# A two-block transformer kernel: one fewer expert round goes through scratch, and the sums read back are added ahead of the last round

## The chip, the core and the metric

The kernel runs on one core of one Trainium2 chip. The metric is the device time of one execution in microseconds (us), lower is better. Engines are called PE (TensorE), ACT (ScalarE), DVE (VectorE), POOL (GpSimd) and SP (SyncE, which here only issues transfers).

## The reference, cut to what matters

Two transformer blocks over 256 tokens of width 1024. The change lies in the last part of the second block, a mixture of experts: every token picks 2 of 32 experts, each expert is a small gated network, and the two results are added with their weights.

```
def hier_moe(h, w_rg, b_rg, w_re, b_re, w1e, w3e, w2e):
    ...
    out = jnp.zeros_like(t)
    for e in range(N_EXPERTS):
        he = jax.nn.silu(t @ w1e[e]) * (t @ w3e[e])
        out = out + cw[:, e:e + 1] * (he @ w2e[e])
    return out.reshape(bsz, seq, d)
```

Behind it stand only `x = x + gt2 * moe`, a last norm (`modulate(rmsnorm_2(x, g_final), shf, scf)`) and the output.

## The kernel before, in words

The 512 (token, expert) pairs are sorted by expert. They are worked off in 20 **rounds** (`NR`), two experts of up to 64 pairs at a time, in the order of the table `ROUNDS`; rounds whose entry is 16 or more take what did not fit into an expert's first 64. A round's weights are six tiles of 1 MB (three for the entry 19): four for gate and up, two for down. They stream from HBM into 15 places, nearly all through SP's queue, in the order of `expert_loads`; a tile is issued when PE has read what lay in its place.

For round i PE makes **gate/up** in two halves (`pe_gate_up`, line 2939, 16 matmuls each), ACT the silu and DVE the product, PE **turns** the hidden tile (`pe_turn_hidden`, line 2961), ACT copies it, and PE makes the **down** product (`pe_down`, line 2973) into two PSUM banks. PE's order interleaves the rounds: first half of i, turn of i-1, second half of i, down of i-1.

What follows a down product depends on `SENT`:

- Rounds below `SENT` go through **scratch**. ACT and DVE copy the two banks to SBUF (lines 3021 and 3066), POOL scatters the rows to a table `Z` in HBM (line 3143; `slot_rows` in the profile), one row per pair. At the end SP reads the whole table back in two transfers (the **readback**, line 3128, into `ZB[0]` and `ZB[1]`, part of the big tile `AR`). ACT multiplies `ZB[0]` by the first weight (line 3053), DVE adds `ZB[1]` times the second (line 3103), and `pe_tokens` (line 2996, 32 matmuls) adds these sums into the PSUM banks of the result.
- Rounds from `SENT` on never leave the core. ACT and DVE make the weighted high and low part of the output (`OHL`, lines 3031 and 3072), DVE a selection matrix (`RT` in the tile `GT`, line 3091), and `pe_back` (line 2984, 16 matmuls) adds the rows to the result's banks.

`ZB` lies where two weight places were, so the readback waits until PE has read the first half of round 18, and for all scatters. Behind the last `pe_back`, DVE adds the result to the residual (line 3299), and the last norm follows. Each engine runs its instructions in the order written, and a wait holds all that is written behind it on that engine. The last round is number 19; "gate/up 19" and so on name its parts.

Of the kernel before, what the change touches and what calls it, by code (L numbers as in the profile page):

```python
# [6 lines left out]
ALU = mybir.AluOpType  # L7
ACT = mybir.ActivationFunctionType
# [26 lines left out]
ROUNDS = (0, 1, 2, 3, 16, 4, 5, 6, 17, 7, 8, 9, 18, 10, 11, 12, 19, 13, 14, 15)  # L35
NR = len(ROUNDS)
WSLOTS = 15
SENT = 17


def tiles(i):
# [164 lines left out]
def build(nc, W, S, K, XI, POS, OUT):  # L206
    with ExitStack() as ctx:
# [72 lines left out]
        p_gu, a_silu, v_mul, a_ah, v_al, p_dn, p_res, v_x = signals("p_gu a_silu v_mul a_ah v_al p_dn p_res v_x")  # L280
# [37 lines left out]
        p_mr, v_mr, a_mr, g_mr = signals("p_mr v_mr a_mr g_mr")  # L318
# [10 lines left out]
        d_zero, d_back = d_ring[2], d_ring[3]  # L329
# [200 lines left out]
        def pe_last_norm(pe, q):  # L530
            q.wait_ge(a_os, SENT + 2 * (NR - SENT))
            q.wait_ge(v_os, SENT + 2 * (NR - SENT))
            for k in range(8):
# [1998 lines left out]
        st8 = get(8 * 2).rearrange("p (n a) -> p n a", a=2)  # L2532
# [42 lines left out]
        ZB = [AR[:, o:o + SLOT].rearrange("p (a d) -> p a d", a=2) for o in (4096, 6144)]  # L2575
# [3 lines left out]
        U0, D0 = 88, 84  # L2579
        row0 = rows.index(("moea", 0))  # L2580
        loads = expert_loads()
        zeroed, back = [16 * sum(1 for s in range(len(order)) if s % RING == b) for b in (2, 3)]
# [360 lines left out]
        def out_read(q, i, n):  # L2943

            if i < SENT:
                q.wait_ge((a_os, v_os)[n], i + 1)
# [4 lines left out]
        def turned(i):  # L2951

            return 4 if i == NR - 1 else 6

        def pe_turn_hidden(pe, q, i):

            q.wait_ge(v_mul, U0 + i + 1)
            if i and turned(i) == 6:
                out_read(q, i - 1, 0)
            for c in range(2):  # L2960
                m = pe.transpose(ps[:, turned(i), c * 128:c * 128 + 128], HID[:, i % 2, c * 128:(c + 1) * 128], ident)
            m.then_inc(*q.up(p_th))

        def pe_down(pe, q, i):

            q.wait_ge(a_ah, U0 + i + 1)
            w = weights(q, i, 2)
            for n in range(2):
                if i:
                    out_read(q, i - 1, n)  # L2970
                for c in range(2):
                    for j in tiles(i):
                        m = pe.matmul(ps[64 * j:64 * j + 64, 6 + n, :], HT[:, i % 2, c, 64 * j:64 * j + 64], w[j][:, c * 1024 + n * 512:c * 1024 + n * 512 + 512],  # L2973
                                      start=c == 0, stop=c == 1, skip_group_check=True)
                m.then_inc(*q.up(p_dn))
# [15 lines left out]
        def pe_tokens(pe, q):  # L2991

            for a in range(2):
                q.wait_ge(v_mr, 12 + a)
                for c in range(8):
                    pe.matmul(half_bank(0, c)[:, 128 * a:128 * a + 128], ZB[0][:, a, c * 128:(c + 1) * 128], ident, start=False, stop=False, skip_group_check=True)

        def pe_experts(pe, q):
            pe_gate_up(pe, q, 0, 0)
            pe_gate_up(pe, q, 0, 1)  # L3000
            pe_rows(pe, q)
            for i in range(1, NR):
                pe_gate_up(pe, q, i, 0)
                pe_turn_hidden(pe, q, i - 1)
                if i - 2 >= SENT:
                    pe_back(pe, q, i - 2)
                pe_gate_up(pe, q, i, 1)
                pe_down(pe, q, i - 1)
            pe_turn_hidden(pe, q, NR - 1)
            pe_back(pe, q, NR - 2)  # L3010
            pe_down(pe, q, NR - 1)
            pe_tokens(pe, q)
            pe_back(pe, q, NR - 1)

        def act_expert_out(act, q, i):
# [17 lines left out]
        def act_experts(act, q):  # L3033
            for i in range(NR + 2):
                if i >= 2:
                    act_expert_out(act, q, i - 2)
                if i + 1 < NR:
                    act_tokens(act, q, i + 1, 0, 8)
                if 1 <= i <= NR:
                    u = i - 1  # L3040
                    q.wait_ge(p_th, u + 1)
                    if u >= 2:
                        q.wait_ge(p_dn, D0 + 2 * (u - 2) + 2)
                    act.activation(acc[:, u % 2, :], ps[:, turned(u), 0:256], ACT.Copy).then_inc(*q.up(a_ah))
                if i < NR:
                    q.wait_ge(p_gu, U0 + 2 * i + 2)
                    if i >= 2:
                        q.wait_ge(p_th, i - 1)
                    act.activation(HID[:, i % 2, :], ps[:, 4 + i % 2, 0:256], ACT.Silu).then_inc(*q.up(a_silu))  # L3049
                if i == NR:  # L3050
                    for a in range(2):
                        q.wait_ge(d_back, back + 32)
                        act.activation(ZB[0][:, a, :], ZB[0][:, a, :], ACT.Copy, scale=st8[:, 6, a:a + 1]).then_inc(*q.up(a_mr))
                if i == 0:
                    q.wait_ge(d_zero, zeroed + 16)
                    for n, x in enumerate((S12, C12)):
                        q.wait_ge(p_mr, 4 + n)
                        act.activation(x, ps[:, n, :], ACT.Copy).then_inc(*q.up(a_mr))
# [16 lines left out]
        def dve_round(v, q, i):  # L3075

            r = ROUNDS[i]
            q.wait_ge(a_mr, 4)
            q.own()
            v.tensor_scalar(EQ, S12, idv[:, r:r + 1], None, ALU.is_equal).then_inc(*q.up(v_own))  # L3080
            q.own()
            if i < SENT:
                v.tensor_tensor_reduce(out=EQ, in0=EQ, in1=slot1, scale=1.0, scalar=0.0, op0=ALU.mult, op1=ALU.add, accum_out=zrow[:, i:i + 1]).then_inc(*q.up(v_own))
                q.own()
                v.tensor_scalar(zno[:, i:i + 1], zrow[:, i:i + 1], 0.0, 4096.0, ALU.is_equal, ALU.mult).then_inc(*q.up(v_own))
                q.own()
                v.scalar_tensor_tensor(out=zidx[:, i:i + 1], in0=zno[:, i:i + 1], scalar=-1.0, in1=zrow[:, i:i + 1], op0=ALU.add, op1=ALU.add).then_inc(*q.up(v_rm))
                return
            if i >= SENT + 2:
                q.wait_ge(p_sc, i - SENT - 1)  # L3090
            v.tensor_tensor(RT[:, i % 2, :], EQ[:, 0:256], EQ[:, 256:512], ALU.add).then_inc(*q.up(v_rm))
            q.wait_ge(a_mr, 5)
            q.own()
            v.tensor_tensor_reduce(out=EQ, in0=EQ, in1=C12, scale=1.0, scalar=0.0, op0=ALU.mult, op1=ALU.add, accum_out=M[:, r:r + 1]).then_inc(*q.up(v_rm))

        def dve_experts(v, q):
            for i in range(NR + 2):
                if i >= 2:
                    dve_expert_out(v, q, i - 2)
                if i == NR:  # L3100
                    for a in range(2):
                        q.wait_ge(a_mr, 6 + a)
                        v.scalar_tensor_tensor(out=ZB[0][:, a, :], in0=ZB[1][:, a, :], scalar=st8[:, 7, a:a + 1], in1=ZB[0][:, a, :], op0=ALU.mult, op1=ALU.add).then_inc(*q.up(v_mr))
                if i == 0:
                    q.wait_ge(a_silu, U0 + 1)
                    v.tensor_tensor(HID[:, 0, :], HID[:, 0, :], ps[:, 4, 256:512], ALU.mult).then_inc(*q.up(v_mul))
                    dve_round(v, q, 0)
                elif i < NR:
                    dve_round(v, q, i)
                    q.wait_ge(a_silu, U0 + i + 1)  # L3110
                    v.tensor_tensor(HID[:, i % 2, :], HID[:, i % 2, :], ps[:, 4 + i % 2, 256:512], ALU.mult).then_inc(*q.up(v_mul))  # L3111

        def sync_experts(sp_, q):

            for m, (i, x, j) in enumerate(loads):
                r = ROUNDS[i]
                if r < PAIRS:
                    place_free(q, m)
                    if i >= 3:
                        q.wait_ge(*read(i - 3, x))  # L3120
                    sp_.dma_start(place(m), W[row0 + 3 * (2 * r + j) + x]).then_inc((d_wa, d_wb, d_wd)[x][i % 3], 16)
                if m == 4:
                    q.wait_ge(g_mr, 1)
                    sp_.dma_start(Z.rearrange("(p a) (b d) -> p (a b) d", p=P, b=2), zeros.unsqueeze(1).broadcast_to([P, 8, 512])).then_inc(d_zero, 16)
            q.wait_ge(p_gu, U0 + 2 * (SENT + 1) + 1)
            q.wait_ge(d_sent, 16 * SENT)
            for c in range(2):
                sp_.dma_start(ZB[c], Z[c * T:(c + 1) * T].rearrange("(a p) d -> p a d", a=2)).then_inc(d_back, 16)
# [340 lines left out]
```

## Time and profile before

| | |
|---|---|
| median of 3 runs | 1602.01 us (1597.74, 1602.01, 1602.54) |
| profiled execution, its time | 1597.53 us |
| profiled execution, its span | 1595.7 us |
| PE busy | 1532.6 us, 96% |
| DVE, ACT, POOL busy | 1057.4, 749.0, 47.9 us |

The span runs from the first to the last instruction, and all times below count from its start. PE's clock is told as granted share of full speed: 1.00 is 2.4 GHz and 0.50 is 1.2 GHz. The change touches only the last 60 us or so.

### The profile page before, as it was taken

The numbers are of one execution on the slowest core, as the hardware profiler recorded it, in microseconds if no ns is written. First come the engines' busy times: TensorE is split into PE (matmuls) and PEld (weight loads), VectorE is DVE, ScalarE is ACT, GpSimd is POOL, SyncE is SP. The second block draws the span as 40 slices with busy tenths as digits, with TensorE's granted clock in tenths as the row PEclk, the third lists the DMA queues.
The fourth block names the chain that finished last, engine by engine and source line by source line (L and its number), as shares of the span: only waits on it lengthen the run. The fifth ranks groups of instructions, "written<-read, shape, count | busy, mean of one in ns | idle before, by whom it ended". The sixth has DMA issues, their size and how long they took to land.

```text
span 1595.7 us, 29188 instructions
## 1 busy us (share of the span) xinstructions
PE 1532.6 (96%) x12098; PEld 1324.7 (83%) x12098; DVE 1057.4 (66%) x2091; ACT 749.0 (47%) x1552; POOL 47.9 (3%) x62
## 2 busy tenths in 40 slices
PE   7999999999999999999989999999999999998897
PEld 7999987889999999998879999999979894332234
DVE  7677775787877787778787787777796546221223
ACT  7455465565444554546365544464744233221124
POOL 0000001000000000000000000000000000222100
PEclk9999999999999999999999999999999999999998
DMA  9746643044666456655314656634410197999993
GB/s 357 282 165 259 263 186 132 1 185 167 244 260 268 174 210 265 263 223 237 122 57 192 240 220 272 251 131 176 147 48 3 54 369 296 417 416 417 418 420 162
DMA packets 55140, 357.75 MB, mean 224 GB/s; under 512 B 9653, under 2 KB 9909, under 8 KB 13152
## 3 DMA queue, kind: packets, MB, share of 16 engines
q1 hardware_dynamic: 48960, 344.92, 54.3%
q0 software_dynamic: 5472, 9.11, 1.5%
q8 instruction: 95, 1.56, 0.4%
q10 hardware_dynamic: 576, 1.86, 0.3%
q14 instruction: 37, 0.30, 0.1%
HBM read 365.64 MB, written 12.06 MB: 237 GB/s over the span
## 4 chain that ended last, share of the span: by engine, by line
PE 82%; DMA 7%; DVE 6%; ACT 3%; issue 1%; SPq 0%; ACTq 0%; DVEq 0%; POOLq 0%
PE ps L433 21%; PE ps L434 21%; PE ps L435 21%; PE ps L2939 5%; DMA AR<-in_w 5%; PE ps L2973 2%; DMA AR<-slot_rows 1%; PE ps L2115 1%; PE ps L1186 1%; ACT SQ L1120 1%; DVE WL L420 1%; PE ps L2687 1%; DVE HL L638 1%; PE ps L1098 1%; PE ps L1153 1%
## 5 line engine op out<-in xcount | busy, mean ns | idle before, releaser
L433 PE MATMUL ps<-HH,WH 128*128 128x256 f32 x1696 | 480.1, 283 | 16.4 <-DVE WL L420 11.6
L420 DVE TENSOR_TENSOR WL<-ring,WH 128x512 fp32r<-128x512 f32 x728 | 451.1, 685 | 52.0 <-ACT WH L409 44.9
L434 PE MATMUL ps<-HL,WH 128*128 128x256 f32 x1696 | 477.9, 282 | 0.0
L435 PE MATMUL ps<-HH,WL 128*128 128x256 f32 x1696 | 477.9, 282 | 0.0
L409 ACT ACTIVATE WH<-ring 128x512 fp32r<-128x512 f32 x728 | 395.5, 621 | 88.1 <-PE ps L435 65.8
L433 PEld LDWEIGHTS ps<-HH,WH 128*128 128x128 f32 x1696 | 320.0, 189 | 19.4 <-DVE HL L638 14.5
L434 PEld LDWEIGHTS ps<-HL,WH 128*128 128x128 f32 x1696 | 320.0, 189 | 0.1
L435 PEld LDWEIGHTS ps<-HH,WL 128*128 128x128 f32 x1696 | 319.9, 189 | 0.0
L433 PE MATMUL ps<-AH,WH 128*128 128x256 f32 x704 | 198.4, 282 | 0.2 <-DVE AL L810 0.2
L434 PE MATMUL ps<-AL,WH 128*128 128x256 f32 x704 | 198.1, 281 | 0.0
L435 PE MATMUL ps<-AH,WL 128*128 128x256 f32 x704 | 198.1, 281 | 0.0
L767 ACT ACTIVATE AF<-AF 128x256 f32<-128x256 f32 x86 | 35.9, 417 | 286.6 <-DVE AF L806 286.6
L433 PEld LDWEIGHTS ps<-AH,WH 128*128 128x128 f32 x704 | 132.5, 188 | 0.5 <-DVE AL L810 0.4
L434 PEld LDWEIGHTS ps<-AL,WH 128*128 128x128 f32 x704 | 132.5, 188 | 0.0
L435 PEld LDWEIGHTS ps<-AH,WL 128*128 128x128 f32 x704 | 132.5, 188 | 0.0
L806 DVE TENSOR_TENSOR AF<-ps,RS 128x512 f32<-128x512 f32 x86 | 59.5, 692 | 50.9 <-PE ps L435 45.0
L3111 DVE TENSOR_TENSOR HID<-HID,ps 128x256 f32<-128x256 f32 x19 | 8.0, 421 | 102.5 <-ACT HID L3049 102.5
L808 DVE TENSOR_TENSOR AF<-AF 128x256 f32<-128x256 f32 x86 | 36.6, 425 | 46.1 <-ACT AF L767 46.1
L2939 PE MATMUL ps<-AR 128*64 128x512 f32 x240 | 65.9, 596 | 0.0
L2939 PE MATMUL ps<-AR,XWR 128*64 128x512 f32 x224 | 62.5, 596 | 2.8 <-DMA AR<-in_w 2.3
L810 DVE TENSOR_TENSOR AL<-AF,AH 128x256 fp32r<-128x256 f32 x86 | 36.6, 425 | 41.6 <-ACT AH L771 41.6
L2973 PE MATMUL ps<-AR,acc 128*64 128x512 f32 x216 | 59.7, 603 | 4.4 <-DMA AR<-in_w 4.4
(565 smaller groups left out, 2189.9 us busy)
## 6 DMA issues: line engine op xcount, KB each, us to landing
ring<-in_w SPq DMA_DIRECT2D x248, 1024.0 KB, 6.9
AR<-in_w SPq DMA_DIRECT2D x70, 1024.0 KB, 20.7
cols<-in_s SPq DMA_DIRECT2D x1, 2994.0 KB, 12.7
SQ<-in_w SPq DMA_DIRECT2D x4, 512.0 KB, 6.4
slot_rows<-RG SPq DMA_DIRECT2D x1, 2048.0 KB, 21.3
AR<-slot_rows SPq DMA_DIRECT2D x2, 1024.0 KB, 19.7
cons<-in_k ACTq DMA_DIRECT2D x1, 1634.0 KB
XT<-in_x SPq DMA_DIRECT2D x2, 512.0 KB
```

Of the source, the lines that this page charges most:

```text
L409: act.activation(hi(n)[:, c * 512:c * 512 + 512], ring[:, i % RING, c * 512:c * 512 + 512], ACT.Copy).then_inc(*q.up(a_wh))
L420: ins = v.tensor_tensor(lo(n)[:, s], ring[:, i % RING, s], hi(n)[:, s].bitcast(F32), ALU.subtract)
L433: pe.matmul(out, ah, bh, start=start, stop=False, skip_group_check=skip)
L434: pe.matmul(out, ah, bl, start=False, stop=False, skip_group_check=skip)
L435: return pe.matmul(out, al, bh, start=False, stop=stop, skip_group_check=skip)
L638: ins = v.scalar_tensor_tensor(out=HL[:, k, :], in0=XT[:, k, :], scalar=gain[:, k:k + 1], in1=HH[:, k, :].bitcast(F32), op0=ALU.mult, op1= ...
L767: act.activation(AF[:, si, 0, :], AF[:, si, 0, :], ACT.Silu).then_inc(*q.up(a_silu))
L806: v.tensor_tensor(AF[:, si], ps[:, b, :].rearrange("p (a t) -> p a t", a=2), RS[:, :].unsqueeze(1).broadcast_to([P, 2, T]), ALU.mult).then ...
L808: v.tensor_tensor(AF[:, si, 0, :], AF[:, si, 0, :], AF[:, si, 1, :], ALU.mult).then_inc(*q.up(v_mul))
L810: v.tensor_tensor(AL[:, si, :], AF[:, si, 0, :], AH[:, si, :].bitcast(F32), ALU.subtract).then_inc(*q.up(v_al))
L2939: m = pe.matmul(ps[64 * j:64 * j + 64, 4 + i % 2, :], XWR[i % 2][:, k, 64 * j:64 * j + 64], w[j][:, (k % 4) * 512:(k % 4) * 512 + 512], st ...
L2973: m = pe.matmul(ps[64 * j:64 * j + 64, 6 + n, :], HT[:, i % 2, c, 64 * j:64 * j + 64], w[j][:, c * 1024 + n * 512:c * 1024 + n * 512 + 512 ...
```

## The change

`SENT` falls from 17 to 16, so round 16 takes the path of `pe_back`. `pe_tokens` is written ahead of the turn of round 19 in PE's program. ACT's two multiplications of `ZB[0]` move from behind the last copy of a turned tile to ahead of the silu of round 19, and DVE's two additions from behind the outputs of round 18 to ahead of the product of round 19. The readback's wait for PE is written in another way and has the same value; its wait for the scatters is for 16 in place of 17.

```diff
-SENT = 17
+SENT = 16
...
             for i in range(1, NR):
...
+            pe_tokens(pe, q)
             pe_turn_hidden(pe, q, NR - 1)
             pe_back(pe, q, NR - 2)
             pe_down(pe, q, NR - 1)
-            pe_tokens(pe, q)
             pe_back(pe, q, NR - 1)
...
+                if i == NR - 1:
+                    for a in range(2):
+                        q.wait_ge(d_back, back + 32)
+                        act.activation(ZB[0][:, a, :], ZB[0][:, a, :], ACT.Copy, scale=st8[:, 6, a:a + 1]).then_inc(*q.up(a_mr))
                 if i < NR:
                     q.wait_ge(p_gu, U0 + 2 * i + 2)
...
                     act.activation(HID[:, i % 2, :], ps[:, 4 + i % 2, 0:256], ACT.Silu).then_inc(*q.up(a_silu))
-                if i == NR:
-                    for a in range(2):
-                        q.wait_ge(d_back, back + 32)
-                        act.activation(ZB[0][:, a, :], ZB[0][:, a, :], ACT.Copy, scale=st8[:, 6, a:a + 1]).then_inc(*q.up(a_mr))
...
-                if i == NR:
-                    for a in range(2):
-                        q.wait_ge(a_mr, 6 + a)
-                        v.scalar_tensor_tensor(out=ZB[0][:, a, :], in0=ZB[1][:, a, :], scalar=st8[:, 7, a:a + 1], in1=ZB[0][:, a, :], op0=ALU.mult, op1=ALU.add).then_inc(*q.up(v_mr))
...
                 elif i < NR:
                     dve_round(v, q, i)
+                    if i == NR - 1:
+                        for a in range(2):
+                            q.wait_ge(a_mr, 6 + a)
+                            v.scalar_tensor_tensor(out=ZB[0][:, a, :], in0=ZB[1][:, a, :], scalar=st8[:, 7, a:a + 1], in1=ZB[0][:, a, :], op0=ALU.mult, op1=ALU.add).then_inc(*q.up(v_mr))
                     q.wait_ge(a_silu, U0 + i + 1)
...
-            q.wait_ge(p_gu, U0 + 2 * (SENT + 1) + 1)
+            q.wait_ge(p_gu, U0 + 2 * (NR - 2) + 1)
             q.wait_ge(d_sent, 16 * SENT)
```

PE at the end of its program: the turn (L2961), `pe_back` (L2984), down (L2973) and `pe_tokens` (L2996) of the last rounds, as a difference.

```order
 L2939 MATMUL ps<-ring,XWR 64x512 x8
 L2973 MATMUL ps<-AR,acc 64x512 x8
+L2996 MATMUL ps<-cons,AR 128x128 x16
 L2961 MATMUL ps<-cons,HID 128x128 x2
 L2984 MATMUL ps<-GT,OHL 128x256 x16
 L2973 MATMUL ps<-AR,acc 64x512 x8
-L2996 MATMUL ps<-cons,AR 128x128 x16
 L2984 MATMUL ps<-GT,OHL 128x256 x16
 L536 MATMUL ps<-cons,SQ 128x1 x16
```

The tokens' matmuls now stand ahead of the turn, the `pe_back` of round 18 and the down product of round 19; before, they stood behind all three.

ACT at the same place, before and then with the change: silu (`HID<-ps`), outputs (`OHL`), copy of a turned tile (`acc`), multiplication of what was read back (`AR<-AR 128x1024`).

```order
L3044 ACTIVATE acc<-ps 128x256
L3049 ACTIVATE HID<-ps 128x256
L3031 ACTIVATE OHL<-ps,AR 128x512 x2
L3044 ACTIVATE acc<-ps 128x256
L3053 ACTIVATE AR<-AR 128x1024 x2
L3031 ACTIVATE OHL<-ps,AR 128x512 x2
L542 ACT_TABLE_LOAD
```

```order
L3044 ACTIVATE acc<-ps 128x256
L3048 ACTIVATE AR<-AR 128x1024 x2
L3053 ACTIVATE HID<-ps 128x256
L3031 ACTIVATE OHL<-ps,AR 128x512 x2
L3044 ACTIVATE acc<-ps 128x256
L3031 ACTIVATE OHL<-ps,AR 128x512 x2
L542 ACT_TABLE_LOAD
```

The pair that waits for the readback now stands ahead of the silu of round 19 (L3053 with the change, L3049 before), of the outputs of round 18 and of the copy of the last turned tile; before, only the outputs of round 19 stood behind it.

The third place is PE's program at round 18, where round 16's `pe_back` is new.

```order
 L2939 MATMUL ps<-AR 64x512 x8
 L2961 MATMUL ps<-cons,HID 128x128 x2
+L2984 MATMUL ps<-GT,OHL 128x256 x16
 L2939 MATMUL ps<-AR 64x512 x8
 L2973 MATMUL ps<-ring,acc 64x512
```

It stands between the halves of gate/up 18, ahead of the down product of round 17.

## Rows read from the trace of the kernel before

**Rows 1.** The page: DMA share and GB/s in 40 slices.

```profile
DMA  9746643044666456655314656634410197999993
GB/s 357 282 165 259 263 186 132 1 185 167 244 260 268 174 210 265 263 223 237 122 57 192 240 220 272 251 131 176 147 48 3 54 369 296 417 416 417 418 420 162
```

**Rows 2.** The chain that ended last, in order: start, us, what.

```profile
1543.88 7.26 DMA slot_rows<-SENDS,AR
...
1551.65 21.82 DMA AR<-slot_rows
1573.47 0.02 issue
1573.50 1.16 ACT AR L3053
1574.65 0.02 issue
1574.68 1.29 DVE AR L3103
1575.97 0.04 issue
1576.02 3.84 PE ps L2996 x32
1579.86 0.48 PE ps L2984 x4
1580.34 0.02 issue
1580.36 0.89 DVE XT L3299 x2
```

**Rows 3.** Timeline of SP's queue: start, us, line, transfer.

```profile
1534.83 8.21 SPq L3121 DMA_DIRECT2D AR<-in_w  x4
1551.22 0.90 SPq L3128 DMA_DIRECT2D AR<-slot_rows  x2
```

**Rows 4.** SP's waits between 1543.1 and 1551.3.

```profile
SPq L169 <- DMA slot_rows<-SENDS,AR: 8.1, 1, 8.1
```

**Rows 5.** Weight transfers issued from 1510 on: time to landing.

```profile
DMA to landing us min/median/max: 23.8/25.5/27.1
```

**Rows 6.** Stretches: busy of PE, PEld, DVE, ACT, POOL; PEclk, DMA share, GB/s.

```profile
1545.00:1551.00 6.00, 6.00 (x28) 1.98 (x28) 0.42 (x1) 0.77 (x2) 0.00 (x0) 1.00 1.02 415
1551.00:1558.00 7.00, 6.90 (x37) 3.02 (x34) 1.99 (x3) 1.76 (x3) 0.00 (x0) 1.00 1.01 419
1558.00:1565.00 7.00, 6.00 (x33) 2.53 (x33) 1.55 (x4) 0.38 (x1) 0.00 (x0) 1.00 1.00 413
1565.00:1568.40 3.40, 3.40 (x22) 1.82 (x19) 1.14 (x2) 1.65 (x3) 0.00 (x0) 1.00 0.68 276
1568.40:1573.50 5.10, 4.97 (x26) 2.04 (x24) 0.36 (x1) 0.00 (x1) 0.00 (x0) 1.00 0.33 131
```

**Rows 7.** Timeline of PE, rounds 18 and 19: start, us, line, idle before.

```profile
1545.53 0.44 PE L2961 MATMUL ps<-cons,HID 128*128 128x128 f32 x2
1549.38 0.59 PE L2973 MATMUL ps<-ring,acc 128*64 128x512 f32 x1
...
1556.67 0.44 PE L2961 MATMUL ps<-cons,HID 128*128 128x128 f32 x2
1556.86 2.15 PE L2984 MATMUL ps<-GT,OHL 128*128 128x256 f32 x16
1558.94 3.65 PE L2939 MATMUL ps<-ring,XWR 128*64 128x512 f32 x16
1563.60 3.65 PE L2973 MATMUL ps<-AR,acc 128*64 128x512 f32 x16 [1.00 <-DMA AR<-in_w]
1567.18 0.44 PE L2961 MATMUL ps<-cons,HID 128*128 128x128 f32 x2
1567.38 2.53 PE L2984 MATMUL ps<-GT,OHL 128*128 128x256 f32 x16
1569.84 3.65 PE L2973 MATMUL ps<-AR,acc 128*64 128x512 f32 x16
```

**Rows 8.** Timelines of ACT and DVE at the readback and at outputs.

```profile
1562.64 0.38 ACT L3049 ACTIVATE HID<-ps 128x256 f32<-128x256 f32 x1 [5.11 <-PE ps L2939]
1573.50 2.19 ACT L3053 ACTIVATE AR<-AR 128x1024 f32<-128x1024 f32 x2 [5.24 <-DMA AR<-slot_rows]
1575.59 1.24 ACT L3031 ACTIVATE OHL<-ps,AR 128x512 fp32r<-128x512 f32 x2
1553.75 0.75 DVE L3072 SCALAR_TENSOR_TENSOR OHL<-ps,AR,OHL 128x512 fp32r<-128x512 f32 x1 [0.89 <-ACT OHL L3031]
1577.08 1.40 DVE L3072 SCALAR_TENSOR_TENSOR OHL<-ps,AR,OHL 128x512 fp32r<-128x512 f32 x2
```

**Rows 9.** PE alone about an idle time: busy, PEclk, DMA share, GB/s.

```profile
1447.90:1451.60 3.70, 0.20 (x4) 1.00 1.01 423
1451.70:1455.10 3.40, 3.40 (x10) 0.50 1.04 417
```

## The prediction

> **What bounds the kernel now.** I read the page's slices first, then the chain that ended last, then each engine's timeline in the last 60 us. PE is busy for 96% of the span, but that says little about the end: the change moves nothing ahead of 1530 us. There the DMA rows of the page matter. In the five slices ahead of the last, the DMA engines are full at 416 to 420 GB/s [rows 1]: the experts' weights stream, and PE waits for them now and then. The chain says what ends last: the scatter of round 16, the readback, which takes 21.82 us from issue to landing at 1573.47, ACT's multiplication, DVE's addition, PE's tokens, the last `pe_back`, the residual at 1580.36 [rows 2]. All that follows the residual (the last norm, the output) is in line behind it, so I count the change by how it moves that 1580.36.
>
> The reader should see two different things in the readback. First, its issue: SP stood 8.1 us for the scatter of round 16 [rows 4] and issued at 1551.22 [rows 3]. Second, its landing: the transfer has 2.1 MB, which at 418 GB/s takes 5.0 us, yet it took over 21. It stood behind weights. Weight transfers of this stretch land 23.8 to 27.1 us after their issue [rows 5], and the last was issued by 1543.04, the end of a group that began at 1534.83 [rows 3]; so the last weights land between about 1566 and 1570. From 1551 to 1573.5 the DMA engines moved 7 x 419 + 7 x 413 + 3.4 x 276 + 5.1 x 131 = 7.4 MB [rows 6]; less the readback's 2.1 MB, 5.3 MB of weights were ahead of it.
>
> **The change part by part.**
>
> *Round 16's scatter is gone, and the readback is issued earlier.* SP now waits for the scatter of round 15 (issued one round of 10.8 us earlier, so landed by about 1540.4) and for the first half of gate/up 18, which ends ahead of the turn at 1545.53 [rows 7]. It issues at about 1545.2 in place of 1551.22, 6 us earlier. At 1545.2 the DMA engines have 5.8 x 415 = 2.4 MB more of weights to move [rows 6], 7.7 MB in all, and no transfer that is issued later stood between the readback and the weights: all weights were issued ahead of it before, and are now. If one queue is served in its order, the bytes ahead of the readback end when they did, and it lands at 1573.5 as before. I take 1573.5, at an effect of nothing for the earlier issue. The cover is the queue of weights itself. The other end of this term is that the landing moves with the issue, 6.0 us earlier; the rows are nearer to the first, since the DMA share is 1.00 to 1.02 until 1565 with the readback already issued [rows 6], and a transfer served at once would have been over by 1557.
>
> The Trainium skill has a rule on this: "DMA: Bandwidth & Descriptors", section "Queues, rings and completion order", says that on each DMA engine the descriptors of one queue are consumed in ring order, and that an engine takes turns between different queues. Both readback and weights are on SP's queue. By that rule the landing stays where it is, and the trace agrees, with weights landing 23.8 to 27.1 us after issue.
>
> *One more `pe_back`, for round 16.* 16 matmuls, 2.15 us, between the halves of gate/up 18 [rows 7]. PE waited 1.00 us for weights ahead of the down product of round 18 at 1563.60 [rows 7], so some 1.0 of the 2.1 is absorbed, and this down product starts at about 1564.6 and ends at 1568.2. Nothing after it can start until the readback is there, so the rest is hidden too. If that cover were gone it would cost 1.1 us. ACT and DVE have the heavier outputs in place of copies (0.7 and 0.75 us each, twice [rows 8]), with idle time of 2 to 5 us a round to hide in: nothing.
>
> *The tokens go ahead of the last round.* This is the term that counts. ACT's pair waits for the readback, and behind it in ACT's order stand the silu of round 19, the outputs of round 18 and the copy of the turned tile 19. Before, that silu ran at 1562.64 and the down product of round 19 at 1569.84, **while** the readback was under way [rows 7, 8]. Now they come after. From the landing on:
>
> 1. ACT and DVE as before: tokens start on PE at 1576.02 and take 3.84, to 1579.86 [rows 2].
> 2. Meanwhile ACT ends its pair at 1575.69, makes the silu (0.38) and the outputs of round 18 (1.24), to 1577.3; DVE the product (0.42) and its outputs (1.40), to 1579.0 [rows 8]. Ready before PE asks.
> 3. Turn of round 19 and `pe_back` of round 18. From a turn to what follows the `pe_back`: 1556.67 to 1558.94, 2.27, or 1567.18 to 1569.84, 2.66 [rows 7]. I take 2.3, to 1582.2.
> 4. Down product of round 19 and its outputs. The like in round 17: down starts at 1549.38 [rows 7], DVE's second output ends at 1553.75 + 0.75 = 1554.50 [rows 8]: 5.1 us. So the residual can start at 1587.3; by then the first half of `pe_back` 19 is done.
>
> That is 1587.3 - 1580.36 = **+7.0 us**, with 2.66 in step 3 +7.3.
>
> *The clock.* PE has now nothing to do between 1568.2 and 1576.0, 7.8 us; before, 2.5 us, at a granted 1.00. In the row for comparison PE stood from 1447.95 to 1451.45 waiting for weights, and the next 3.4 us ran at 0.50, 1.2 GHz [rows 9]. A fall is likelier after the longer stand; it may begin before 1576.0, and what is left of it costs half of its length. Bounds: nothing, and, if the whole 3.4 lies behind 1576 and a second such stretch follows, 3.4. I take 1.3, less than half of the longer bound, because PE works hard from 1576.0 on.
>
> "TensorE: Matmul & The Clock Gate" in the Trainium skill, section "What's actually happening", states that the half rate is the default and comes back with idleness, and that activity releases it. By it the term would be between nothing and a few us, as I have it; the trace agrees, with its 0.50 after an idle 3.5 us.
>
> **Sum:** 7.0 + 1.3 = +8.3 us against the profiled execution's own 1597.53: 1605.8. That execution lies at the low end of the runs shown (1597.74, 1602.01, 1602.54), 4.5 below their median; I add the sum to the median, 1602.01 + 8.3 = **1610.3**.
>
> **Rivals.**
>
> *A, the readback lands as much earlier as it is issued* (1567.5). For it: the release of SP really comes 6 us earlier, and the DMA share falls to 0.68 from 1565 on [rows 6]. Against: 7.7 MB of weights are ahead. Then the chain of steps 1 to 4 starts 6.0 earlier, tokens at 1570.0, with an idle time too short for much of a fall: 7.0 - 6.0 = +1.0, 1603.0. Chance 0.10.
>
> *B, not slower: the readback overtakes the weights and lands before 1565.6.* Then the order of PE decides alone: tokens from 1568.2, 3.84, to 1572.0; turn and `pe_back` 2.3; down and outputs 5.1; residual at 1579.4, 0.9 **earlier** than 1580.36, 1601.1. The point of decision is a landing at 1566.5, 7.0 earlier than now. Against it: the DMA engines show no room. It is also the best this order can give. Chance 0.04.
>
> *C, the clock stays at 1.00 through the idle time.* +7.0, 1609.0; chance 0.15. *D, a longer stretch at 0.50 or a later landing* (round 19's weights late, step 3 at its longer end): 7.3 + 3.4 = +10.7, 1612.7; chance 0.15. The forecast with its middle clock term: 0.56. C, D and it are the same mechanism.
>
> **How the numbers follow.** The mechanism holds in 0.86 of the cases, at +7.0 to +10.7. 0.3% is 4.8 us, about what a measurement of this kernel can tell from no change. The runs before spread over 4.8 us by themselves; if the new ones fall at the low end and the old at the high end, a true +8.3 shows as +3.5. I move 0.14 of the 0.86 to "within" for that, and with A and B this gives slower 0.72, same 0.24; faster 0.04, which is B with a lucky draw. The range runs from A's 1603 less a little for the runs' spread (1602) to D's 1612.7 (1613).
>
> **What the changed profile would show.** SP's readback issued near 1545 with about 28 us to landing, at 1573 to 1574: right. A landing near 1567.5 or earlier: A or B, and the prediction is wrong. Silu 19 on ACT behind the pair that waits, at about 1575.7 in place of 1562.6. PE idle 7 to 8 us ahead of line 2996, with a granted clock of 0.50 in part of what follows. `pe_back` 16 in line 2984 (64 matmuls in place of 48 in the last stretch). The residual at 1587 to 1589. What would make it wrong beyond the landing: a wait of ACT or DVE that I have as ready and that comes last on PE's chain, or the weights of round 18 or 19 landing at other times than in this execution.

## The result, and the profile after

The changed kernel takes 1607.47 us (median of 7 runs, 1605.3 to 1608.37) against 1601.4 for the kernel before (7 runs, 1597.74 to 1602.54). The ratio is 1.0044, 95% interval 1.0031 to 1.0056, which is 5 to 9 us more: slower, by a little. The profiled executions have spans of 1604.1 and 1595.7 us, 8.4 apart.

The chain that ended last in the changed kernel (start, us, what) answers to [rows 2]:

```profile
1545.71 0.39 SPq L3128
...
1546.14 27.38 DMA AR<-slot_rows
...
1573.54 1.16 ACT AR L3048
...
1574.72 1.30 DVE AR L3109
...
1576.07 6.30 PE ps L2996 x32
1582.36 0.22 PE ps L2961 x2
1582.58 1.90 PE ps L2984 x16
1584.48 3.61 PE ps L2973 x16
...
1588.11 0.70 ACT OHL L3031
...
1588.84 0.75 DVE OHL L3072
1589.59 0.80 DVE XT L3299 x2
...
1591.09 3.75 PE ps L536 x32
```

Three things are to be seen. The readback was issued at 1545.71, 5.5 us earlier than in [rows 3], and landed at 1573.52, where it landed before (1573.47): the time from issue to landing (of the second of its two transfers, which lands last) grew from 21.8 to 27.4 us. Behind the tokens (L2996) there are now the turn, a `pe_back`, the down product and its outputs, which in [rows 2] were not in the chain. And the tokens took 6.30 us in place of 3.84. The residual starts at 1589.59 in place of 1580.36, 9.2 us later.

The traces also show when the readback's data moved. Its rows are pieces of 4 KB, the weights' are of 8 KB. Of pieces under 8 KB the DMA engines moved 4 to 8 in each us from 1556 to 1559, then 17, 28 and 36 in the next three with the change, and 16, 31 and 39 before it. So the first rows of the readback moved at about 1559 in both executions, whether it was issued at 1545.7 or at 1551.2. The last landed at 1573.5, 14.5 us later and not the 5.0 us that 2.1 MB need at 418 GB/s. From 1559 on rows and weights were mixed, and the DMA share fell from 1.00 (1558 to 1565) over 0.68 to 0.33 [rows 6], so a part of the DMA engines was done while others still had work.

ACT's timeline of the changed kernel (start, us, line, idle before), which answers to [rows 8]:

```profile
1558.80 0.39 ACT L3044 ACTIVATE acc<-ps 128x256 f32<-128x256 f32 x1 [3.11 <-PE ps L2961]
1573.54 2.19 ACT L3048 ACTIVATE AR<-AR 128x1024 f32<-128x1024 f32 x2 [14.36 <-DMA AR<-slot_rows]
1575.64 0.36 ACT L3053 ACTIVATE HID<-ps 128x256 f32<-128x256 f32 x1
1575.90 1.25 ACT L3031 ACTIVATE OHL<-ps,AR 128x512 fp32r<-128x512 f32 x2
```

ACT stands 14.36 us for the readback, with the silu of round 19 (before at 1562.64) and the outputs of round 18 behind it. PE alone in stretches of the same execution: busy, granted clock, DMA share, GB/s.

```profile
1567.70:1571.00 3.30, 0.00 (x0) 1.00 0.50 201
1571.00:1576.00 5.00, 0.00 (x0) 0.50 0.07 29
1576.10:1581.20 5.10, 5.10 (x24) 0.50 0.00 0
1581.30:1584.70 3.40, 3.40 (x30) 1.00 0.00 0
```

PE is done with round 18 at 1567.7 and has nothing until 1576.07. Its clock fell to 0.50 (1.2 GHz) at 1571.0 and came back at 1581.2, so 5.1 us of matmuls ran at half speed.

### The profile page after: what moved, and what is told of

It is laid out like the page before. It is cut to its first block, busy times and chain, and to the rows that moved or that the text cites. A ratio compares the mean times of both kernels' runs of the same rounds, so it can differ in the third digit from the quotient of the medians.

```text
span 1604.1 us, 29217 instructions
## 1 busy us (share of the span) xinstructions
PE 1535.6 (96%) x12114; PEld 1328.0 (83%) x12114; DVE 1057.6 (66%) x2091; ACT 749.6 (47%) x1553; POOL 46.9 (3%) x61
## 4 chain that ended last, share of the span: by engine, by line
PE 82%; DMA 7%; DVE 6%; ACT 3%; issue 1%; ACTq 0%; SPq 0%; DVEq 0%
PE ps L433 21%; PE ps L435 21%; PE ps L434 21%; PE ps L2939 5%; DMA AR<-in_w 5%; PE ps L2973 3%; DMA AR<-slot_rows 2%; PE ps L2115 1%; PE ps L1186 1%; ACT SQ L1120 1%; DVE WL L420 1%; PE ps L2687 1%; DVE HL L638 1%; PE ps L1098 1%; PE ps L1153 1%
## 5 line engine op out<-in xcount | busy, mean ns | idle before, releaser
L433 PE MATMUL ps<-HH,WH 128*128 128x256 f32 x1696 | 480.1, 283 | 16.5 <-DVE WL L420 11.6
L433 PEld LDWEIGHTS ps<-HH,WH 128*128 128x128 f32 x1696 | 319.9, 189 | 19.5 <-DVE HL L638 14.5
L433 PE MATMUL ps<-WH,HH 128*128 128x512 f32 (+2 forms) x160 | 62.3, 389 | 1.2 <-DVE HL L638 1.2
```

The source lines that it names most:

```text
L433: pe.matmul(out, ah, bh, start=start, stop=False, skip_group_check=skip)
```

## The experiments

Executions differ by up to some 4.5 us in what lies ahead of the last 60 us, all engines alike. So I compare times within each kernel's own profile: from the readback's landing to the residual, and from PE's turn of round 17 (1545.53 in [rows 7]) to the residual. That turn stands ahead of all that the change moves on PE, so the second is a common scale for all kernels. The ratio to the kernel before stands beside them.

| kernel | issue to landing | landing to residual | turn of round 17 to residual | tokens | ratio (95%) |
|---|---|---|---|---|---|
| before | 21.8 | 6.9 | 34.8 | 3.84 | |
| changed | 27.4 | 16.1 | 44.0 | 6.30 | 1.0044 (1.0031 to 1.0056) |
| only 16 rounds | 27.4 | 6.9 | 34.8 | 3.84 | 1.0004 (0.9991 to 1.0018) |
| only the order | 21.6 | 16.3 | 44.1 | 6.51 | 1.0043 (1.0029 to 1.0057) |
| only PE's order | 27.4 | 15.5 | 43.4 | 5.69 | 1.0050 (1.0031 to 1.0068) |
| only ACT's and DVE's order | 27.4 | 17.1 | 45.0 | 3.84 | 1.0065 (1.0040 to 1.0089) |
| ACT's queue | 18.6 | 18.1 | 37.7 | 3.84 | 1.0023 (1.0012 to 1.0034) |
| PE kept busy | 27.3 | 13.6 | 41.5 | 3.84 | 1.0038 (1.0025 to 1.0050) |
| no readback | none | none | 33.1 | 3.84 | 0.9993 (0.9979 to 1.0007) |
| halves, on the kernel before | 20.6 | 5.1 | 33.1 | 2.05 + 2.05 | 0.9981 (0.9968 to 0.9993) |

### Only 16 rounds through scratch

```diff
-SENT = 17
+SENT = 16
...
-            q.wait_ge(p_gu, U0 + 2 * (SENT + 1) + 1)
+            q.wait_ge(p_gu, U0 + 2 * (NR - 2) + 1)
```

> Only SENT = 16, the order of the tokens as before. My theory (the order costs all, the earlier issue gives nothing): readback issued near 1545.7, landing at 1573.4 to 1573.5 as in both traces, residual at 1580.4 plus or minus 0.2, time within 1 us of before. Rival (the extra pe_back or the heavier outputs of round 16 cost something themselves): residual 1 to 2 us later. Second rival (the earlier issue is worth something that the new order hides): residual up to 6 us earlier.

The chain of this kernel:

```profile
1547.82 0.39 SPq L3128
...
1548.24 27.38 DMA AR<-slot_rows
...
1575.64 1.16 ACT AR L3053
...
1576.82 1.29 DVE AR L3103
...
1578.16 3.84 PE ps L2996 x32
1582.00 0.49 PE ps L2984 x4
...
1582.51 0.89 DVE XT L3299 x2
```

The absolute times missed, since this execution is 2 us later already when the readback is issued (1547.82 against 1545.71). From issue to landing it is 27.4 us as in the changed kernel, and from landing to residual 6.9 as before. The landing comes 27.9 us after the turn of round 17, as in the kernel before and in the changed one, and the residual 34.8 us after it, as before. The ratio is 1.0004 (0.9991 to 1.0018), which by itself leaves room for up to 3 us. In the profile neither the extra `pe_back` nor the earlier issue moves the residual.

### Only the order

The changed kernel with `SENT = 17`.

> Only the new order, SENT = 17 kept. My theory: the readback is issued near 1551.2 and lands at 1573.5; residual at 1589 to 1590, as in the changed kernel, time 8 us over before. Rival (the two parts of the change add up, each with some microseconds): residual 2 us or more earlier than in the changed kernel.

From its chain:

```profile
1552.14 0.39 SPq L3128
...
1552.56 21.60 DMA AR<-slot_rows
...
1576.71 6.51 PE ps L2996 x32
...
1590.46 0.79 DVE XT L3299 x2
```

The issue was at 1552.14, the landing at 1574.17, the residual at 1590.46: 16.3 us from landing to residual, and a ratio of 1.0043 beside 1.0044. The order is the whole loss.

### Which engine's order

Two halves of the move, each with `SENT = 16`. First PE's alone, shown against the changed kernel: ACT's pair goes behind the outputs of round 18 and ahead of the copy of the turned tile 19, since PE turns that tile only behind the tokens, which need the pair. DVE's pair goes back behind the outputs of round 18 (not shown).

```diff
+                if i == NR:
+                    for a in range(2):
+                        q.wait_ge(d_back, back + 32)
+                        act.activation(ZB[0][:, a, :], ZB[0][:, a, :], ACT.Copy, scale=st8[:, 6, a:a + 1]).then_inc(*q.up(a_mr))
                 if 1 <= i <= NR:
                     u = i - 1
...
-                if i == NR - 1:
-                    for a in range(2):
-                        q.wait_ge(d_back, back + 32)
-                        act.activation(ZB[0][:, a, :], ZB[0][:, a, :], ACT.Copy, scale=st8[:, 6, a:a + 1]).then_inc(*q.up(a_mr))
```

> SENT = 16, PE's tokens ahead of the turn of round 19, but ACT's and DVE's pairs stand behind the silu, product and outputs of round 18, so only PE waits. My theory: PE's order alone costs all, since turn, pe_back 18 and down 19 (5.9 us of PE) and the outputs come behind the tokens: residual at 1589.6 plus or minus 0.5 as in the changed kernel. Rival (the silu of round 19 held on ACT is what costs): residual near 1580.4.

Then ACT's and DVE's alone: the tokens go back behind the down product.

```diff
-            pe_tokens(pe, q)
             pe_turn_hidden(pe, q, NR - 1)
             pe_back(pe, q, NR - 2)
             pe_down(pe, q, NR - 1)
+            pe_tokens(pe, q)
             pe_back(pe, q, NR - 1)
```

> SENT = 16, ACT's and DVE's pairs early as in the change, PE's tokens behind down 19 as before. My theory: PE waits for the product of round 19 until 1577.5 and for the outputs of round 18 until 1578.9, then pe_back 18, down 19, tokens, pe_back 19 follow one another: residual at 1590 to 1592, later than in the changed kernel, since the tokens no longer run while DVE works. Rival (only PE's order counts): residual near 1580.4.

ACT's and PE's timelines of the first kernel, which landed at 1577.08:

```profile
1567.84 0.38 ACT L3053 ACTIVATE HID<-ps 128x256 f32<-128x256 f32 x1 [5.11 <-PE ps L2939]
1577.11 2.19 ACT L3042 ACTIVATE AR<-AR 128x1024 f32<-128x1024 f32 x2 [5.15 <-DMA AR<-slot_rows]
1579.63 5.69 PE L2996 MATMUL ps<-cons,AR 128*128 128x128 f32 x32 [8.40 <-DVE AR L3103]
```

PE's timeline of the second kernel, which landed at 1576.16:

```profile
1580.23 0.69 PE L2961 MATMUL ps<-cons,HID 128*128 128x128 f32 x2 [9.91 <-DVE HID L3111]
1580.58 3.89 PE L2984 MATMUL ps<-GT,OHL 128*128 128x256 f32 x16
1584.39 4.59 PE L2973 MATMUL ps<-AR,acc 128*64 128x512 f32 x16
1588.92 3.84 PE L2996 MATMUL ps<-cons,AR 128*128 128x128 f32 x32
```

Either half alone costs as much as both. With PE's alone, the silu and the outputs of round 18 were in time (the silu at 1567.84, 9 us ahead of the landing), and still 15.5 us passed from landing to residual. With ACT's and DVE's alone, PE waited 9.91 us for the product of round 19, and the tokens had to follow the down product: 17.1 us. Taken from the landing, my theory expected 15.6 to 16.6 and 16.5 to 18.5 us: the second held, the first was missed by 0.1. The landings are 3.6 and 2.7 us later than expected, since these executions were. Both rivals fell: it isn't one engine's wait that costs, but that the last round is behind the readback in any way.

### The readback on ACT's queue

```diff
+                if i == NR - 2:
+                    q.wait_ge(p_gu, U0 + 2 * (NR - 2) + 1)
+                    q.wait_ge(d_sent, 16 * SENT)
+                    for c in range(2):
+                        act.dma_start(ZB[c], Z[c * T:(c + 1) * T].rearrange("(a p) d -> p a d", a=2)).then_inc(d_back, 16)
...
-            for c in range(2):
-                sp_.dma_start(ZB[c], Z[c * T:(c + 1) * T].rearrange("(a p) d -> p a d", a=2)).then_inc(d_back, 16)
```

> The changed kernel, but the readback is issued by ACT on its own queue, at the same moment (behind the first half of gate/up 18). My theory (the readback lands late because SP's queue serves the weights ahead of it in order): landing 10 to 14 us after issue, near 1557 to 1560, the last weights up to 5 us later; tokens follow down 18 on PE without idle time, residual near 1583, 6 us earlier than in the changed kernel but some 3 us later than before, since the last down product now waits for its weights and stands behind the tokens. Rival (the readback waits for something else, for example the DMA engines as a whole): landing at 1573.5 whatever the queue, time as the changed kernel.

ACT's issue and its wait, from its timeline, and PE's wait for the weights:

```profile
1550.55 0.92 ACTq L3049 DMA_DIRECT2D AR<-slot_rows  x2
1569.65 2.19 ACT L3053 ACTIVATE AR<-AR 128x1024 f32<-128x1024 f32 x2 [5.50 <-DMA AR<-slot_rows]
```

```profile
1567.32 3.65 PE L2939 MATMUL ps<-ring,XWR 128*64 128x512 f32 x16 [1.69 <-DMA ring<-in_w]
1573.12 3.65 PE L2973 MATMUL ps<-AR,acc 128*64 128x512 f32 x16 [2.14 <-DMA AR<-in_w]
1576.70 3.84 PE L2996 MATMUL ps<-cons,AR 128*128 128x128 f32 x32
```

The landing came 18.6 us after the issue in place of 27.4, so 8.8 us of the wait came from the place in SP's queue behind the weights, and the rival fell. The size was missed: I had 10 to 14. The Trainium skill, "DMA: Bandwidth & Descriptors", section "Queues, rings and completion order", says that a DMA engine takes turns between the queues that have work for it. The trace agrees: between 1555 and 1568 ACT's queue moved 482 pieces with 1.91 MB and SP's queue 481 pieces with 3.51 MB. The numbers are equal, as they are when turns are taken piece by piece, and the readback, with pieces half as long, had about a third of the bytes, 147 GB/s. That is the size I missed. What the readback gained the weights lost: PE now waits 1.69 and 2.14 us for them, where the changed kernel did not, and this execution was 4.5 us late when the last rounds began (turn of round 17 at 1550.07 against 1545.59). With that taken off, the residual (1587.77) is 6.3 earlier than in the changed kernel and 2.9 later than before, as expected; the ratio of 1.0023 is half the loss. The 18.1 us from landing to residual in the table are no wait for the readback: PE goes from the down product of round 18 to the tokens with no gap, and what it waited for were weights. Early data does not help an order in which tokens and last round are still one line on PE.

### PE kept busy

```diff
+            pe_keep32(pe, 4, 8)
             pe_tokens(pe, q)
             pe_turn_hidden(pe, q, NR - 1)
```

> The changed kernel with 8 matmuls of 128x512 on constants ahead of the tokens, into a free bank, their result unused. My theory (2.5 us of the loss are the clock's fall in the idle time): granted clock 1.00 through the tokens, tokens in 3.84 us in place of 6.30, from landing to residual 13.4 to 13.9 us in place of 16.1. Rival (the tokens are slow for another reason, for example the reads of AR behind DVE's writes): still 6.3 us.

PE's timeline of this kernel, and stretches of it (as above):

```profile
1568.39 7.13 PE L1126 MATMUL ps<-cons 128*128 128x512 f32 x16
1576.78 3.84 PE L2996 MATMUL ps<-cons,AR 128*128 128x128 f32 x32 [1.26 <-DVE AR L3110]
```

```profile
1568.40:1575.50 7.10, 7.10 (x18) 1.00 0.29 115
1576.80:1580.60 3.80, 3.80 (x35) 1.00 0.00 0
```

The 8 matmuls stand as x16 because the trace records each of these twice; in the same way the 32 records of the tokens are 16 matmuls as written. The clock stayed at 1.00, the tokens took 3.84 us, and from landing to residual it was 13.6 us in place of 16.1: 2.5 us of the loss were the clock. The rival, that the reads of `AR` slow the tokens, fell. The run times alone can't show this: 1.0038 (1.0025 to 1.0050) overlaps the changed kernel's 1.0044, and 0.4 us of the 2.5 were lost again behind the residual, where the 32 small matmuls (L536) took 4.11 us in place of 3.75.

### No readback

```diff
-            for c in range(2):
-                sp_.dma_start(ZB[c], Z[c * T:(c + 1) * T].rearrange("(a p) d -> p a d", a=2)).then_inc(d_back, 16)
...
-                        q.wait_ge(d_back, back + 32)
+                        q.wait_ge(p_gu, U0 + 2 * (NR - 2) + 1)
```

> The changed kernel without the readback: ACT's pair waits for the first half of gate/up 18 and works on what lies in the places, so what rounds 0 to 15 give is left out of the result. My theory (the order itself costs nothing once the landing is early; all hangs on the landing): tokens directly behind down 18, residual at 1578 to 1579.5, time 1 to 2 us under before. Rival (ACT's and DVE's new order costs something even so): residual later than before.

Part of its chain:

```profile
1567.89 3.43 PE ps L2973 x16
1571.32 3.77 PE ps L2996 x32
1575.09 0.22 PE ps L2961 x2
1575.31 1.90 PE ps L2984 x16
1577.21 3.61 PE ps L2973 x16
```

The tokens follow the down product with no gap. The residual is at 1582.31 in an execution that is 3.6 us late at the turn of round 17 (1549.23 against 1545.59), so 1578.7 on the changed kernel's scale: 1.7 under before. The ratio, 0.9993 (0.9979 to 1.0007), can't tell that from no change. Its lower end bounds what the new order could give with the landing out of the way: 3.4 us at most, and 1.7 by the profile.

### The readback in halves, on the kernel before

Since the order gives nothing, I tried the line behind the landing itself, in the old order.

```diff
-            for c in range(2):
-                sp_.dma_start(ZB[c], Z[c * T:(c + 1) * T].rearrange("(a p) d -> p a d", a=2)).then_inc(d_back, 16)
+            for a in range(2):
+                for c in range(2):
+                    sp_.dma_start(ZB[c][:, a, :], Z[c * T + a * P:c * T + a * P + P]).then_inc((d_back, d_half)[a], 16)
...
-                        q.wait_ge(d_back, back + 32)
+                        q.wait_ge(*((d_back, back + 32), (d_half, 32))[a])
```

> The kernel before, with the readback cut by rows: four transfers of 0.5 MB, both tables' first 128 rows ahead, with a semaphore for each half, so that ACT's and DVE's first piece and 16 of the 32 matmuls run while the second half comes in. My theory (what stands behind the landing is one line, so only the second half's share of it should stay): from the last landing to the residual 5.0 us in place of 6.9. Rival (the first half lands hardly earlier, since the slowest DMA engine sets both): 6.0 to 6.9 us.

PE's timeline of this kernel:

```profile
1570.71 3.65 PE L2975 MATMUL ps<-AR,acc 128*64 128x512 f32 x16
1574.37 2.05 PE L2998 MATMUL ps<-cons,AR 128*128 128x128 f32 x16
1576.91 2.05 PE L2998 MATMUL ps<-cons,AR 128*128 128x128 f32 x16 [0.48 <-DVE AR L3105]
```

The first half of the tokens (16 of the 32 records) ran straight behind the down product. ACT could start on the first half at 1571.85; the second half landed at 1574.36, 28.0 us after the turn of round 17 (27.9 before), and the residual came 5.1 us later in place of 6.9. The rival fell: the first half was there some 2.5 us ahead of the second. The ratio is 0.9981 (0.9968 to 0.9993), 1 to 5 us less than the kernel before: faster by a little, and the only one here that is. Between its two groups of tokens PE still waits 0.48 us.

## Why the prediction was right

It gave 1610.3 us in a range of 1602 to 1613; measured were 1607.47. The mechanism held step by step; two sizes in it, the clock's and that of the new `pe_back` on PE, were off.

- *The landing.* Forecast: issue near 1545.2, landing at 1573.5. Profile: 1545.71 and 1573.52. The kernel with only 16 rounds has the same 27.4 us from issue to landing, and the one on ACT's queue shows that 8.8 of them come from the place in SP's queue. Rivals A and B, which needed an earlier landing, did not come true. The kernel without a readback shows that B's gain would have been small, but about twice what I made it: 0.9 forecast, 1.7 in the profile.
- *One more `pe_back`.* Forecast: nothing at the residual. Shown by the kernel with only 16 rounds: 6.9 us from landing to residual as before. On PE I let 1.1 of its 2.1 us reach the down product of round 18 and measured 0.4 (from the turn of round 17, 18.50 us with the change and 18.07 before). So PE was free at 1567.7 and not at 1568.2, which is most of what rival B's gain was short of.
- *The last round behind the tokens.* Forecast +7.0. In the chain: turn and `pe_back` 2.12, down to the second output 5.11, less the 0.50 that the old chain had between tokens and residual, 6.7. I had taken 2.3 for the first.
- *The clock.* Forecast +1.3, measured 2.5 (6.30 less 3.84; 16.1 less 13.6 with PE kept busy). This is the term that was mis-sized: I took less than half of the longer bound because "PE works hard from 1576.0 on", but 5.1 us of that work ran at 0.50 all the same. The measured 2.5 lie within the bound of 3.4.
- *What follows the residual.* I took it as moved in one piece. It gave back 0.7 us: the 32 small matmuls of the norm's sum took 3.75 us in place of 4.43 ([rows 2] end just ahead of them). Before, they began at 1581.96 and the clock was at 0.50 from 1584.8 on, in their midst; with the change they began at 1591.09 and it was at 1.00 until about 1594.9, just past their end. So +9.2 at the residual became +8.4 in the span, against a forecast of 8.3: two misses of opposite sign, not precision.

The median moved by 6.1 us and the profiled span by 8.4; the interval, 5 to 9 us, holds the forecast sum. I had also added the sum to a median of three runs, 1602.01, that became 1601.4 with seven. So of the 2.8 us between forecast and measurement 0.6 is the base, and 2.2 is that the medians moved by less than the two profiled executions; the spread of the runs, 4.8 us before, covers that, and no run here says more about it.

## What to carry to other kernels

Here an issue that moved ahead by 5.5 us did not move the landing, since, by the prediction's sum, some 7.7 MB stood ahead of it in its queue: look at bytes ahead and time to landing, not at the wait that was shortened. On an engine that works in order, put what waits for the last transfer behind all that can run without it, on every engine of the line; either of two engines in the wrong order was enough to lose the whole. If a result must come last, cut the transfer and its followers in pieces, so that only the last piece's share is left behind the landing.

## What the runs showed that I had not expected

- PE was idle from 1567.7, its clock fell at 1571.0, and it stayed at 0.50 for 5.1 us after matmuls had begun again at 1576.07. In the kernel with PE's order alone that was 3.9 us. With ACT's and DVE's order alone it was 6.1 us, and the `pe_back` at 1580.58 took 3.89 us in place of 2.15.
- The second of the two issues of the readback took 3.63 us of SP's time when issued at 1546.1, and 0.47 when issued at 1551.6. SP had nothing else to do. On ACT's queue, with about as much outstanding on SP's, both issues of the readback took under 0.5 us.
- On ACT's queue the readback was slower than I had it (18.6 us). Its share of the bytes (35% between 1555 and 1568) accounts for 14 to 15 us of that for 2.1 MB. Another 3 us are that its first piece moved at about 1554.0, 3 us after the second issue at 1551.0; what held it until then no run here shows.
- Equal code ahead of the last rounds ended up to 4.5 us apart between executions. In the kernel with only 16 rounds, a stretch at 0.50 lasted from 1453.4 to 1460.2, twice as long as in [rows 9], but that is not the cause of its later start: the turn of round 5 was already 2.1 us late (1401.83 against 1399.75), and the turn of round 17, behind the stretch, 2.2. On ACT's queue, 4.4 of the 4.5 us were there at the turn of round 5. Where they come from no run here shows.
